# Dense products that stream the two token halves in turn

## The reference

```python
for i in range(DEPTH):                       # layer 0: gated short convolution, layer 1: windowed attention
    hp, hs = rmsnorm(xp, norm_mix[i]), rmsnorm(xs, norm_mix[i])
    # layer 0: split(h @ w_in, 3), depthwise conv of width 3, (bg * conv) @ w_out
    # layer 1: h @ w_qkv (4608 columns), q/k norms, three dilated windows, merge, o @ w_out
    xp, xs = xp + mp, xs + ms
    hp, hs = rmsnorm(xp, norm_ffn[i]), rmsnorm(xs, norm_ffn[i])
    # silu(conv(h @ w_gate) + b) * (h @ w_up)) @ w_down, D_FF = 2816
    xp, xs = xp + fp, xs + fs
```

## Time and profile before

| | |
|---|---|
| median of 3 runs | 1292.55 us (1292.3 to 1293.63) |
| span of the profiled execution | 1291.8 us, 28424 instructions |
| PE busy | 1278.6 us (99%), 11567 matmul records |
| DVE busy | 735.8 us (57%) |
| ACT busy | 515.8 us (40%) |
| mean granted clock of TensorE | 0.999 of full speed |
| DMA | 193.22 MB, 150 GB/s |

### The profile page before, as it was taken

The page is one execution under the profiler, slowest core; times in us unless marked ns, Lnnn a source line. Parts: engine busy times, 40 slices in busy tenths (PEclk is TensorE's granted clock), DMA queues, the critical chain, the costliest instruction groups (busy, mean ns, idle before and its releaser), DMA issues.

```text
span 1291.8 us, 28424 instructions
## 1 busy us (share of the span) xinstructions
PE 1278.6 (99%) x11567; PEld 1261.5 (98%) x11567; DVE 735.8 (57%) x1167; ACT 515.8 (40%) x848; POOL 21.1 (2%) x50
## 2 busy tenths in 40 slices
PE   8999999999999999999999999999999999999999
PEld 8999999999999999999999999998999999999998
DVE  6655565556655543334567676768766555663332
ACT  5222244433434332224455465555544343441111
POOL 0000000000000000000000000000000000000000
PEclk9999999999999999999999999999999999999999
DMA  8344534655444544453456756469544444445441
GB/s 220 98 155 141 163 101 143 175 157 163 140 138 127 158 139 149 133 158 118 146 172 191 227 145 207 149 158 255 148 131 136 138 148 146 141 129 170 123 107 40
DMA packets 285301, 193.22 MB, mean 150 GB/s; under 512 B 40393, under 2 KB 281537, under 8 KB 284070
## 3 DMA queue, kind: packets, MB, share of 16 engines
q1 hardware_dynamic: 282092, 137.04, 38.5%
q0 software_dynamic: 1792, 54.43, 11.7%
q10 hardware_dynamic: 1338, 0.61, 0.2%
HBM read 184.52 MB, written 64.16 MB: 193 GB/s over the span
## 4 chain that ended last, share of the span: by engine, by line
PE 94%; DMA 3%; DVE 2%; SPq 1%; ACT 0%; issue 0%; DVEq 0%; ACTq 0%
PE acc L1820 84%; PE acc L1848 2%; DMA skv<-new_rows 1%; PE M L1848 1%; PE N L2085 1%; PE M L1809 1%; PE N L1809 1%; DMA wraw<-in_sc_w_in_dram 1%; PE acc L2065 1%; DMA new_rows<-row_q 1%; PE M L2034 1%; DVE wl L1193 0%; PE acc L2136 0%; PE N L1848 0%; PE acc L2076 0%; SPq L599 0%
## 5 line engine op out<-in xcount | busy, mean ns | idle before, releaser
L1820 PE MATMUL acc<-hh,wh 128*128 128x260 f32 x2256 | 456.8, 284 | 3.6 <-DVE head_ones_r L1657 1.7
L1820 PE MATMUL acc<-hh,wl 128*128 128x260 f32 x2256 | 454.9, 283 | 0.0
L1820 PE MATMUL acc<-hl,wh 128*128 128x260 f32 x2256 | 453.8, 283 | 0.0
L815 ACT ACTIVATE wh<-wraw 128x1024 fp32r<-128x1024 f32 (+1 forms) x211 | 219.4, 1040 | 558.9 <-PE acc L1820 553.0
L1820 PEld LDWEIGHTS acc<-hh,wh 128*128 128x128 f32 x2256 | 347.7, 189 | 5.4 <-DVEq L1548 1.9
L1820 PEld LDWEIGHTS acc<-hh,wl 128*128 128x128 f32 x2256 | 347.8, 188 | 0.0
L1820 PEld LDWEIGHTS acc<-hl,wh 128*128 128x128 f32 x2256 | 346.9, 188 | 0.0
L1193 DVE TENSOR_TENSOR wl<-wraw,wh 128x1024 fp32r<-128x1024 f32 (+1 forms) x211 | 252.9, 1199 | 160.9 <-ACT wh L815 158.0
L1820 PE MATMUL acc<-yh,wh 128*128 128x260 f32 x834 | 169.3, 284 | 1.4 <-DVE x L1714 0.8
L1820 PE MATMUL acc<-yh,wl 128*128 128x260 f32 x834 | 167.7, 282 | 0.0
L1820 PE MATMUL acc<-yl,wh 128*128 128x260 f32 x834 | 167.5, 282 | 0.0
(11 more groups left out here) (253 smaller groups left out, 1025.1 us busy)
## 6 DMA issues: line engine op xcount, KB each, us to landing
out_dram<-in_cache_kv_d_dram POOLq DMA_DIRECT2D x24, 1364.0 KB, 6.4
wraw<-in_ffn_w_gate_dram SPq DMA_DIRECT2D x44, 512.0 KB, 3.9
wraw<-in_ffn_w_up_dram SPq DMA_DIRECT2D x44, 512.0 KB, 4.0
wraw<-in_attn_w_qkv_dram SPq DMA_DIRECT2D x36, 512.0 KB, 4.0
out_dram<-in_cache_kv_d_dram POOLq DMA_DIRECT2D x8, 2044.0 KB, 9.4
wraw<-in_ffn_w_down_dram SPq DMA_DIRECT2D x32, 448.0 KB, 3.9
wraw<-in_sc_w_in_dram SPq DMA_DIRECT2D x24, 512.0 KB, 4.0
wraw<-in_ffn_w_down_dram SPq DMA_DIRECT2D x16, 512.0 KB, 4.6
```

The lines of the kernel that those rows point to most:

```text
L815: nc.scalar.activation(wh[c % 2][:, 0:k], wraw[:, c % 4, 0:k], ACT.Copy).then_inc(hi_done, 1)
L1820: ins = T.matmul(acc[:, par, h2, 0:HALF], w[c % 2][:, k, :], a[:, k0 + k, h2, :], start=(first and k == 0 and n == 0), stop=(last and k == ...
```

## The change

The dense products no longer stream one half of the tokens per matmul. Each of the two matmuls of a pair takes a range of positions n of *both* halves, in the order n of half 0, n of half 1, n + 1 of half 0, and so on. The weights, the number of matmuls and the sum of their columns (520) stay. The first matmul (`b` = 0) takes positions 0 to `cut`, the second the rest. With `ALL_CUT` (130) both have 260 columns; with `ROW_CUT` (128) they have 256 and 264, and then the eight sample columns all lie in the second bank behind 256 prompt columns. `ROW_CUT` is used for the gate chunks, the query, key and value chunks and the last product.

PSUM then holds the halves in turn: word 2n + h2. Every readout takes every second word of each bank for one half (`by_half`, `prompt_by_half`, `sample_by_half`) and writes where it wrote before.

```diff
+        def paired(a, b, cut):
+            lo, hi = ((0, cut), (cut, HALF))[b]
+            return a[:, :, lo:hi].rearrange("p h n -> p n h")
+
+        def pair_bank(bank, b, cut):
+            n = (cut, HALF - cut)[b]
+            return bank[:, b, 0:2 * n].rearrange("p (n h) -> p n h", h=2)
+
+        def by_half(bank):
+            return bank[:, :, 0:HALF].rearrange("p b (n h) -> p h b n", h=2)
+
+        def prompt_by_half(bank):
+            return bank[:, :, 0:HP].rearrange("p b (n h) -> p h b n", h=2)
...
                     for n, (w, a) in enumerate(((wh, xh), (wh, xl), (wl, xh))):
-                        for h2 in range(2):
-                            ins = T.matmul(acc[:, par, h2, 0:HALF], w[c % 2][:, k, :], a[:, k0 + k, h2, :],
+                        for b in range(2):
+                            ins = T.matmul(pair_bank(acc[:, par], b, cut), w[c % 2][:, k, :],
+                                           paired(a[:, k0 + k], b, cut),
...
-                V.tensor_tensor(xm, acc[:, par, :, 0:HALF], xm, ALU.add).then_inc(x_ready, 1)
+                V.tensor_tensor(cut2(xm), by_half(acc[:, par]), cut2(xm), ALU.add).then_inc(x_ready, 1)
...
-                    o = t.rearrange("p (c h n) -> p h n c", c=NCLS, h=2)
-                    V.tensor_tensor(o, a[:, :, 0:HP].rearrange("p h (n c) -> p h n c", c=NCLS),
-                                    prompt(r).rearrange("p h (n c) -> p h n c", c=NCLS), ALU.mult)
+                    o = t.rearrange("p (c h b n) -> p h b n c", c=NCLS, h=2, b=2)
+                    halves = a[:, :, 0:HP].rearrange("p b (n c h) -> p h b n c", c=NCLS, h=2)
+                    for h2 in range(2):
+                        V.tensor_tensor(o[:, h2], halves[:, h2],
+                                        r[:, h2, 0:HP].rearrange("p (b n c) -> p b n c", b=2, c=NCLS), ALU.mult)
...
-            for h2 in range(2):
+            for b in (1, 0):
                 for k in range(k1 - k0):
-                    if h2 and k == 5:
-                        last_transposes(0, M[:, 0, 0:P], M[:, 0, P:2 * P], 0)
+                    if b == 0 and k == 5:
+                        odd_transposes()
```

More of the change, by code:

```diff
@@ L56 @@
 QB = P // NCLS
+ALL_CUT = HALF // 2
+ROW_CUT = HP // 2
 T0W = 2 * P + NCLS
@@ L768, in ahead, with sample_by_half, cut2 @@
             return [(0, c + 2)]
+        def paired(a, b, cut):
[8 more added lines that the diff above has]
+            return bank[:, :, 0:HP].rearrange("p b (n h) -> p h b n", h=2)
+        def sample_by_half(bank):
+            return bank[:, 1, HP:HP + NS].rearrange("p (n h) -> p h n", h=2)
+        def cut2(a):
+            return a.rearrange("p h (b n) -> p h b n", b=2)
         def prompt(a):
@@ L1390, in last_residual_halves @@
             def last_residual_halves():
-                for h2 in range(2):
-                    dve.wait_ge(half_done, h2 + 1)
-                    xm = x[:, DK - 1, h2]
-                    V.tensor_tensor(xm, acc[:, 1, h2, 0:HALF], xm, ALU.add).then_inc(fin_x, 1)
+                for i, (b, lo, hi) in enumerate(((1, ROW_CUT, HALF), (0, 0, ROW_CUT))):
+                    dve.wait_ge(half_done, i + 1)
+                    xm = x[:, DK - 1, :, lo:hi]
+                    V.tensor_tensor(xm, acc[:, 1, b, 0:2 * (hi - lo)].rearrange("p (n h) -> p h n", h=2), xm,
+                                    ALU.add).then_inc(fin_x, 1)
             def ffn(layer, gu, dn, v0, x0, next_norm, rows_n):
@@ L1841, in first_chunk, with k_step @@
                 return {k: (lambda k=k: at(k)) for k in range(DK)}
-            def k_step(dst, c, k, xh, xl, first, last):
+            def k_step(dst, c, k, xh, xl, first, last, cut=ALL_CUT):
                 for n, (w, a) in enumerate(((wh, xh), (wh, xl), (wl, xh))):
-                    for h2 in range(2):
-                        ins = T.matmul(dst[:, h2, 0:HALF], w[c % 2][:, k, :], a[:, k, h2, :],
+                    for b in range(2):
+                        ins = T.matmul(pair_bank(dst, b, cut), w[c % 2][:, k, :], paired(a[:, k], b, cut),
                                        start=(first and n == 0), stop=(last and n == 2))
@@ L1898, in _ @@
                             x_transpose(2)
-                        for h2 in range(2):
-                            T.matmul(acc[:, 0, h2, 0:HALF], w[0][:, 0, :], a[:, 0, h2, :], start=(n == 0), stop=False)
+                        for b in range(2):
+                            T.matmul(pair_bank(acc[:, 0], b, ALL_CUT), w[0][:, 0, :], paired(a[:, 0], b, ALL_CUT),
+                                     start=(n == 0), stop=False)
                 if m == DK - 1:
@@ L1992, in ffn, with down @@
                 ins.then_inc(rows_t, 1)
-                def down(it, c):
+                def down(it, c, cut=ALL_CUT):
                     k0, k1 = DN_CUT[c % 3]
@@ L2013, in ffn @@
                     for c in range(11):
-                        down(1, c)
+                        down(1, c, ROW_CUT if c >= 9 else ALL_CUT)
                     pe.wait_ge(rows_tok, layer + 2)
@@ L2258, in last_output @@
                 for i, (w, a) in enumerate(((wo_h, yh_r), (wo_h, yl_r), (wo_l, yh_r))):
-                    for h2 in range(2):
-                        ins = T.matmul(wo_bank(m)[:, h2, 0:HALF], w[:, m, :], a[:, NP_ - 1, h2, :],
+                    for b in range(2):
+                        ins = T.matmul(pair_bank(wo_bank(m), b, ALL_CUT), w[:, m, :], paired(a[:, NP_ - 1], b, ALL_CUT),
                                        start=(i == 0), stop=(i == 2))
```

83 lines of the change are left out of this document (44 added, 39 removed).

## The result

The changed kernel takes **1220.4 us** (median of 4 runs, 1219.91 to 1221.61) against 1292.42 us for the kernel before on the same chip (median of 4): a ratio of 0.9442, 95% interval 0.943 to 0.9453. The forecast was 1212 us in a range of 1190 to 1320; what came is rival A's case, 8 us above its number.

A forecast was written before the change was run, and what follows sets the result against it. The prediction took the PE's matmul pace to bound the kernel, with 9.2 ns of read stalls per dense matmul. 1291.8 - 90 + 2 + 1 + 6 = 1210.8 us, given as 1212 us since runs lie 0.75 us higher; range 1190 to 1320.

The forecast's parts named there:

- rival A: The forecast itself: the dense matmuls' 9.2 ns loss goes; 1212 us, from 1190 to 1230; chance 0.45.
- The reading of the 9.2 ns: Dense matmuls take 120.0 ns, not 110.8: stalls in reading the moving operand when consecutive words are read at full pace.
- The stream, -90 us: All 9792 dense matmuls lose the 9.2 ns, the lower bound; the upper bound, 219 ns each, was +969 us.
- 256 and 264 columns at 0: Pairs of 256 and 264 columns instead of 260 and 260 still have 520 columns: cost 0.
- Readouts +2: 187 large readouts read PSUM with step 2, exposed mainly in 27 single-bank attention chunks: 0 to 4 us, taken as 2.
- value readouts +1: Eight value chunks' readouts in two pieces pay the fixed part of about 155 ns again: 0 to 1.3 us, counted 1.
- The end at 0: Behind the last product, two transposes instead of three and a last readout of 256 elements: -0.1 us, counted 0.
- Late next, +6 us: In the attention layer the chain leaves the PE for DMAs and VectorE: 6 of about 18 us gain lost.
- B: Half of the dense matmuls' loss goes, distance 115 ns: 1253 us, from 1230 to 1289; chance 0.20.
- C: No change, the port's word rate limits whatever the addresses, distance stays 120 ns: 1292.55 to 1295 us; chance 0.07.
- D: Slower through step-2 readouts, decided in the attention layer's 27 single-bank chunks, PE keeping 120 ns: 1298 to 1320 us; chance 0.11.
- E: Slower stream: full pace needs neighbouring words fetched together, so dense matmuls go to 219 ns: 2261 us; chance 0.17.

The follow-up runs named there:

- the skip order: Changed kernel, both halves still in turn, but all even positions first, then all odd ones: 1298.99 us, ratio 1.0052 to the kernel before.
- the kernel in order: Changed kernel with the read order alone undone, every dense matmul reading its tokens one after the other: 1291.79 us, ratio 0.9994 to the kernel before.
- the kernel with its chunks in order: Changed kernel with the read order undone only in the attention layer's query, key, value and output chunks: 1232.5 us, 12.1 us more than the changed kernel.
- the shifted order: Block of 48 matmuls added to the changed kernel, groups of 8 words read 0, 4, 1, 5, 2, 6, 3, 7 but starting two words later: 117.5 ns per matmul.

## Why the prediction was right, and where it was off

**What bounds the kernel:** right. PE's pace was the time, and nothing but PE's pace moved it.

**The reading of the 9.2 ns:** right in its essence, that consecutive words at full pace stall the read, and it had rested on two arguments that held: the float32 rows and the unequal blocks. The mechanism as put ("each place read at half the pace") was wrong. What counts is the words per stretch and side; the skip order reads each place at half pace too, and loses everything (1298.99 us). The choice of the lower bound rested on this mechanism, with a cover that was called thin. That the order of the change happens to give each side all four words of a stretch was not foreseen, and in this the forecast had luck.

**The stream, -90 us:** mis-sized. It came to 9792 x (120.1 - 112.4) = -75 us. The step that failed is "a dense matmul with the same fixed part would take 110.8 ns". The fixed part is right (215.8 ns for 512 columns, 110.8 with 32 weight columns), but the floor of the load of 128 weight columns, 111.7 ns, was left out: 0.9 ns, 9 us. The other 0.7 ns, 6 us, is the uneven 110 and 114, whose cause is open. No row of the kernel before showed this floor: its transposes, each with a load of 128 weight columns in plain float32, are 110 ns apart, under it.

**256 and 264 columns at 0:** right: 109.7 and 115.0 ns in the changed kernel, 224.7 for the pair; 260 + 260 take 224.8.

**Readouts +2, value readouts +1:** both too high. 692 ns with step 2 and with step 1, and the kernel in order shows less than 1 us for all of it. The slack is used up at the value readout shown above, where the PE waits 0.27 us, but it has grown the stage's idle time by no more than 0.63 us with all else. The bound by the spread store was the wrong neighbour: a store with large steps tells nothing of a PSUM read with step 2.

**The end at 0:** right by the same kernel.

**Late next, +6 us:** too high. The attention layer gained 13.45 us in the profile, and 12.1 of 14.4 by the timing of the kernel with its chunks in order; I had kept two thirds. The DMA chains are there and did become the longest way for 38 us, as predicted. But the PE's idle time in the whole stage grew by 0.63 us only, so it had other work beside them. The step that failed is that a piece of the chain which leaves the PE was charged in full (17 us at 7.7%, three times) as if the PE stood still in it.

**The sum:** the stream 15 us short, the other terms 7 us too dear (about +2 instead of +9), which makes the 8 us between 1212 and 1220. The two errors have opposite signs, so part of the closeness is luck.

**The rivals.** B (115 ns) and C (120 ns, 1292.55 to 1295) would have shown in the windows; the distance is 112.1. D is refuted by 692 ns. There the PSUM part of the rule in the Trainium skill (Advanced Engine Details and Errata, section Memory Cachelines) asks that every two consecutive elements be contiguous; in these readouts every second word costs as much as every word. E, at 2261 us, is refuted, though its pace is real: one word per stretch and side gives 222 to 240 ns. The Trainium skill's rule for SBUF in the same section, lines of 16 bytes and at least two accesses in a row to each, is half of the truth for these matmuls. The 16 bytes agree with the shifted order's row. But changing line at every column is at full pace here (111.7 ns). In the picture of two sides that is because each side takes four words from its line one after the other. And two accesses in a row by each side, which the kernel before had, are not quite enough: by the sizes above a stretch costs a side 1.80 ns and feeds 1.67 ns of columns.

## What to carry to other kernels

Where matmuls in the reduced float type with a moving operand in SBUF bound a kernel, compare the distance between starts with columns / 2.4 + 2.5 ns. If consecutive words are read in order, 7 to 8% of it can be had (120.2 to 111.7 ns for 260 columns, 233.3 to 215.8 for 512; 6.4% in this kernel) by an order that gives even and odd columns four words of one 16-byte stretch each (two places in turn, aligned, near or far), and VectorE can pick the results apart with step 2 in PSUM at the pace of step 1 (692 ns for 512). Up to 260 columns the 111.7 ns with 128 weight columns are the next limit. And a chain that leaves the PE is no loss until the PE's idle time shows one.

## What the runs showed of the hardware

- The in-order read of fp32r words loses 7 to 8%: 120.2 ns for 260 columns, 233.3 for 512, where 111.7 and 215.8 are reached otherwise. In the picture of two sides, and less the fixed 2.5 ns, a new 16-byte stretch costs a side 1.76 to 1.80 ns, whether it takes one word of it (229.2 / 130 and 234.2 / 130) or two (230.8 / 128).
- A step of 2 or 4 words halves the pace, but a step of 32 words is a little faster than these (222 ns for 232 to 237).
- With 128 weight columns fp32r matmuls are 111.7 ns apart in the mean at the least, with 256 streamed columns as with 260; with 32 weight columns they are 109.2 and 110.8 ns apart. Single distances can be shorter: in the changed kernel 109.7 and 115.0 take turns. The transposes in plain float32, with 128 columns and 128 weight columns, are 109.4 ns apart.
- In the same picture a side keeps at least two stretches and fewer than four: 135.4 ns with two in turn for a side, 240 with four. Three was not tried.
